# Products of zeros on TensorE between the first sixteen weight tiles, a later distance table and an earlier sum matrix

## The chip, the cores and the metric

The program runs on one core of one Trainium2 chip. The metric is the device time of one execution in microseconds. Before the change three timed runs took 1464.62, 1458.6 and 1463.09 us, so the median is 1463.09 us.

## What is computed

One inference step of a decoder of two layers, for a prompt of 256 tokens and 8 sample sequences of 8 tokens, with a model width of 1024. Everything is float32. What matters here is how a layer begins:

```python
def adaln(c, w, b):
    m = jax.nn.silu(c) @ w + b
    sh, sc, g = jnp.split(m, 3, axis=-1)
    return sh[:, None], sc[:, None], g[:, None]

def run_layer(x, c, mixer, w_ada_mix_l, b_ada_mix_l, w_in_l, ...):
    sh, sc, g = adaln(c, w_ada_mix_l, b_ada_mix_l)
    h = x * (1 + sc) + sh
    o, state = mixer(split_heads(h @ w_in_l))
...
```

No projection can start before the shift `sh` and the scale `sc` of the first layer are there. They are a product of the 9 conditioning vectors with 2048 of the 3072 columns of `w_ada_mix`, which is 8 MB of weights. A table of biases over distances (32 buckets times 16 heads) is also made once and is added to the logits of all attention maps later.

## The kernel before, in words

The five engines run programs of their own that meet at semaphores. Weights come as tiles of 512 KB. SP loads them in the order of the list `STREAM` into a ring of `RING = 4` slots; the load of tile n waits until tile n-4 has been used (`tile_used`).

**The front** is what stands ahead of the first projection. `FIRST` holds its 16 tiles. Tile n of it is counted from 0 here.

- POOL clears `cz`, then (L645 to L649) `epsc`, `qs`, `qi`, `wall`, `sel`, `selB`, `turnO`, `znew` and `sbias`, and signals `zeroed` once after `cz` and once at the end.
- ACT issues nine small loads (the list `first`, L713), the identity matrix first, then makes the exponential of the conditioning vectors. DVE makes silu of them into `cz` (L1407), padded with zeros to 32 columns.
- PE (`ada_tile`, L994) multiplies: for each tile two matmuls with 32 stationary columns of `cz` and 512 moving columns of the tile, each into a quarter of `bank[3]` by partitions. Two neighbouring tiles of a group of four use four different quarters.
- After each fourth tile ACT copies the bank to `adarow` (`ada_out`, L725), PE turns it in `ada_turn` (L1004: four products of a 128x128 piece of `adarow` with `sumG`, the 128x32 matrix that adds the quarters up), and DVE adds the bias into `adaT` (`ada_add`, L1447 and L1449).
- After tile 3 PE makes the distance table: three products of `relb` (34x16) with 1159 columns (L1025). It waits for all of `first`. DVE copies it out (L1419), and ACT writes it 16 times over to memory at the end of the front (`dist_sample`, L731), 1159 KB.
- `sumG` is made by DVE from the identity with three adds (L1409 to L1416), after a wait for all of `first`; the lambda terms (L1410, L1414) lie between these adds. ACT has the exponential of lambda (L717) ahead of its first `ada_out`.
- POOL and DVE make h of the first layer from `adaT` and x (L663, L666, L1526). PE then starts with the four tiles of `INDEX`: two together in `by_chunks` (L981, 16 matmuls), two in `chunk` (L972), then 16 matmuls with `wki` (L1044), and goes on with the list `PROJ`.

**SP around it** issues tiles 0 to 11, x, tiles 12 to 15, the four tiles of `INDEX` and `wki`. The load of the last `INDEX` tile waits for tile 15 of the front. Then, without any wait for PE, come the page numbers and the page loads of the indexer's keys (`load_ik(l, 0)`, L473), the nine constants (L535), `load_ik(l, 1)`, the loads of PROJ tiles 0 and 1, `load_ik(l, 2)`, and the loads of PROJ tiles 2 and 3. The load of PROJ tile 4 waits for PROJ tile 0 on PE. All of this is in program order, written out by hand.

Of the kernel before, what the change touches and what calls it, by code (L numbers as in the profile page):

```python
# [37 lines left out]
NCOND = 1 + NB  # L38
# [151 lines left out]
def repeat(ap, n):  # L190

    return bass.AP(ap.tensor, ap.offset, [*[list(x) for x in ap.ap], [0, n]])


def program(nc, a, out):
    ctx = ExitStack()
    with ctx:
# [3 lines left out]
        def sem(name):  # L201
            return ctx.enter_context(nc.semaphore(name))
# [38 lines left out]
              for x in (*(big[:, FF // P * T + PAST * s:FF // P * T + PAST * s + PAST] for s in range(6)),  # L241
# [52 lines left out]

        ld_cond = sem("ld_cond")
        ld_first = sem("ld_first")
        ld_x = sem("ld_x")
# [95 lines left out]

        first = [(ident[:], a["ident"]), (par_all[:, :, 0:P_NLAM], a["params"]),
                 (relb[0:32, :], a["rel_bias"]), (relb[32:34, :], a["relrows"]), (onehot, a["onehot"]),
# [50 lines left out]
        def _(sp):  # L446
# [74 lines left out]
            for l in range(DEPTH):  # L521
# [6 lines left out]
                if l == 0:  # L528

                    sp.wait_ge(ld_first, N_FIRST)  # L530
                    load_ik(l, 0)

                    sp.wait_ge(zeroed, 2)
# [107 lines left out]
        def _(pool):  # L641
# [3 lines left out]
            pool.memset(epsc[:], EPS)  # L645
            for t in (qs, qi, wall, sel, selB, turnO, znew, *sbias):
                pool.memset(t[:], 0.0)
# [61 lines left out]
        def _(act):  # L709
            for signal in (z_set, pd_relu, sd_relu, u_tset, up_relu, ln_x):  # L710
                act.sem_inc(signal.sem, signal.spare)
            for dst, src in first:
                act.dma_start(dst, src).then_inc(ld_first, 16)  # L713
            act.wait_ge(ld_cond, 16)
            act.activation(sgm[:], cT[:], ACT.Exp, scale=-1.0).then_inc(sig_exp, 1)
            act.wait_ge(lam_sum, 1)
            act.activation(ls[:], ls[:], ACT.Exp).then_inc(lam_exp, 1)  # L717

# [7 lines left out]

            ada_out(FIRST[3])
            for g in range(1, 4):
                ada_out(FIRST[4 * g + 3])
            act.wait_ge(dist_sb, 3)  # L730
            act.dma_start(dist_s, bass.AP(distb.tensor, distb.offset,  # L731
# [19 lines left out]
            load_ik(5)  # L751
            act.wait_ge(zeroed, 2)

# [196 lines left out]
        def _(pe):  # L950
# [57 lines left out]
            def sums(l, j):  # L1008
# [8 lines left out]
                          ).then_inc(ln_mm.sem, 1)  # L1017

            pe.wait_ge(silu_done, 1)
            for n, t in enumerate(FIRST):  # L1020
                ada_tile(t)
                if n == 3:
                    pe.wait_ge(ld_first, N_FIRST)
                    for c, (u0, u1) in enumerate(((0, 512), (512, 1024), (1024, NDIST))):
                        pe.matmul(bank[c][0:H, 0:u1 - u0], relb[:], big[0:34, u0:u1], start=True, stop=True  # L1025
                                  ).then_inc(dist_ps, 1)
                    pe.wait_ge(sum_set, 1)
                if n >= 4 and n % 4 == 0:
                    ada_turn(n // 4 - 1)
            ada_turn(3)  # L1030
            pe.wait_ge(zeroed, 2)

# [365 lines left out]
        def _(dve):  # L1398
# [7 lines left out]
            dve.wait_ge(zeroed, 1)  # L1406
            dve.tensor_tensor(cz[:, :, 0:NCOND], cT[:], sgm[:], ALU.mult).then_inc(silu_done, 1)  # L1407
            dve.wait_ge(ld_first, N_FIRST)
            dve.tensor_tensor(sumG[:], ident[:, 0:G], ident[:, G:2 * G], ALU.add)  # L1409
# [3 lines left out]
            dve.tensor_tensor(sumG[:], sumG[:], ident[:, 2 * G:3 * G], ALU.add)  # L1413
            dve.tensor_reduce(ls[:], lp, AX_X, ALU.add).then_inc(lam_sum, 1)  # L1414
            dve.drain()
            dve.tensor_tensor(sumG[:], sumG[:], ident[:, 3 * G:4 * G], ALU.add).then_inc(sum_set, 1)  # L1416
            for c, (u0, u1) in enumerate(((0, 512), (512, 1024), (1024, NDIST))):
# [3 lines left out]
            for l in range(DEPTH):  # L1421
# [10 lines left out]
                dve.memset(par_all[0:3 * G, l, P_COEF:P_COEF + 1], 1.0)  # L1432
            dve.wait_ge(zeroed, 2)
# [3 lines left out]
            def ada_add(t):  # L1437

                kind, l, i = t
                j, q = (1 if kind == "mlp" else 0), i // 4  # L1440
                dve.wait_ge(ada_tp, ada_group(t) + 1)
                to = adaT[:, 2 * l + j, 4 * q:4 * q + 4, :]
                ps = bank[4][:, 0:4 * G].rearrange("p (c n) -> p c n", n=G)[:, :, 0:NCOND]
                b0 = P_ADA + 24 * j + 4 * q
                bias = repeat(par_all[:, l, b0:b0 + 4], NCOND)
                if q < 2:
                    ins = dve.tensor_tensor(to, ps, bias, ALU.add)  # L1447
                else:
                    ins = dve.scalar_tensor_tensor(to, ps, 1.0, bias, ALU.add, ALU.add)  # L1449
                ins.then_inc(ada_set, 1)  # L1450

            for g in range(4):
                ada_add(FIRST[4 * g + 3])
# [431 lines left out]
```

## Time and profile before

| What | Value |
|---|---|
| Median of three runs | 1463.09 us (1458.6 to 1464.62) |
| The profiled execution: its time | 1461.34 us |
| Its span in the trace | 1459.3 us |
| Mean granted clock of TensorE | 0.967 |
| PE busy | 1345.6 us, 92% of the span |
| DVE, ACT, POOL busy | 505.3, 287.1 and 62.6 us |
| DMA, mean | 249 GB/s |

All durations below are of the one profiled execution. Its time is 2.0 us above its span, for what lies around the program, and 1.75 us below the median of the timed runs. The front is about 43 us of it. In the rows PE is a matmul, PEld a load of stationary weights, SPq and ACTq the issuing of DMAs on SP and ACT. A float32 matmul appears as two records, so "x16" is eight matmuls.

### The profile page before, as it was taken

How to read it: one execution, taken by the hardware profiler on the slowest of the kernel's cores; microseconds unless marked ns; L12 is line 12 of the kernel's file. 1: busy time of each engine (PE TensorE's matmuls, PEld its weight loads, DVE VectorE, ACT ScalarE, POOL GpSimd, SP SyncE). 2: the span in 40 equal slices, each digit the busy share in tenths (PEclk: the TensorE clock that was granted, in tenths of full speed). 3: DMA queues.
4: the chain of work that ended last, by engine and by line, in shares of the span. 5: the costliest groups of instructions: out<-in, count | busy, mean ns of one | idle time of the engine just before them, and what ended most of it. 6: DMA issues, size and time to landing. Idle time of an engine off the chain costs nothing.

```text
span 1459.3 us, 23536 instructions
## 1 busy us (share of the span) xinstructions
PE 1345.6 (92%) x8190; PEld 852.3 (58%) x8190; DVE 505.3 (35%) x1319; ACT 287.1 (20%) x712; POOL 62.6 (4%) x271
## 2 busy tenths in 40 slices
PE   6989899988899999999999999998879899999996
PEld 2544356655565666566665543665546567767774
DVE  1102777863354011011112077777534611100113
ACT  0011123343213111000003112433432311000001
POOL 1100000000001000000001000000000100000000
PEclk7899999999899999999999999999989999999998
DMA  7788979999943676987672677899994536675663
GB/s 278 208 279 269 306 233 359 357 298 308 293 145 108 238 263 234 320 290 262 264 259 95 209 263 239 303 366 294 298 332 160 195 135 248 214 280 203 237 203 129
DMA packets 189567, 363.82 MB, mean 249 GB/s; under 512 B 22912, under 2 KB 140360, under 8 KB 187786
## 3 DMA queue, kind: packets, MB, share of 16 engines
q1 hardware_dynamic: 165200, 350.19, 69.8%
q10 hardware_dynamic: 24250, 12.14, 3.2%
q8 instruction: 66, 1.08, 0.3%
q14 instruction: 51, 0.42, 0.1%
HBM read 354.17 MB, written 58.40 MB: 283 GB/s over the span
## 4 chain that ended last, share of the span: by engine, by line
PE 67%; SPq 10%; DVE 6%; DMA 6%; issue 5%; DVEq 3%; ACT 2%; ACTq 1%; POOLq 0%; POOL 0%
PE psf L972 21%; PE psf L1383 18%; SPq L473 9%; DMA ring<-in_tiles 4%; PE psf L1260 4%; PE psf L1298 4%; PE psf L1366 3%; PE psf L994 2%; PE psf L981 2%; PE psf L1153 2%; PE psf L1196 2%; DVE m L1515 2%; DVEq L1518 1%; PE psf L1044 1%; PE psf L1295 1%
## 5 line engine op out<-in xcount | busy, mean ns | idle before, releaser
L972 PE MATMUL psf<-hT,ring 128*128 128x320 f32 x1440 | 399.8, 435 | 10.0 <-DMA ring<-in_tiles 8.6
L972 PEld LDWEIGHTS psf<-hT,ring 128*128 128x128 f32 x1440 | 270.3, 190 | 139.4 <-issue 17.8
L1383 PE MATMUL psf<-big,ring 128*128 128x320 f32 x1024 | 279.3, 434 | 2.2 <-DVE big L1731 2.1
L1383 PEld LDWEIGHTS psf<-big,ring 128*128 128x128 f32 x1024 | 193.4, 190 | 88.5 <-issue 4.2
L1731 DVE TENSOR_TENSOR big<-sq 128x320 f32<-128x320 f32 x64 | 31.5, 492 | 261.5 <-ACT sq L941 261.2
L1459 DVE TENSOR_SCALAR rstd<-psf,adaT 128x256 f32<-128x256 f32 x32 | 15.4, 483 | 248.4 <-PE psf L1383 233.3
L1515 DVE MAX8 m<-workbuf 64x8 f32<-64x1032 f32 x64 | 78.5, 1226 | 3.0
L1153 PE MATMUL psf<-big,qs 128*32 128x512 f32 x512 | 69.5, 633 | 8.7 <-issue 5.6
L1517 DVE MATCH_REPLACE8 workbuf<-m,workbuf 64x1032 f32<-64x1032 f32 x64 | 77.4, 1209 | 0.0
L941 ACT ACTIVATE sq<-psf 128x320 f32<-128x320 f32 x64 | 28.0, 438 | 249.7 <-PE psf L972 233.1
L903 ACT ACTIVATE sq<-xT 128x320 f32<-128x320 f32 x32 | 15.1, 470 | 307.1 <-DVE xT L1463 307.1
L994 PE MATMUL psf<-ring,cz 128*32 128x512 f32 x384 | 63.2, 673 | 13.2 <-DVE cz L1407 8.4
L1196 PE MATMUL psf<-big,ptbuf 128*32 128x128 f32 x2048 | 65.4, 282 | 9.5 <-DMA big<-in_pool_cv 9.5
L1260 PE MATMUL psf<-oT,ring 128*128 128x320 f32 x256 | 71.4, 435 | 2.1 <-DVE oT L1622 1.0
L1196 PEld LDWEIGHTS psf<-big,ptbuf 128*32 128x32 f32 x2048 | 56.6, 113 | 16.1 <-issue 14.2
L1298 PE MATMUL psf<-ring,hT 128*128 128x512 f32 x128 | 65.2, 633 | 0.0
L1260 PEld LDWEIGHTS psf<-oT,ring 128*128 128x128 f32 x256 | 48.0, 190 | 23.2 <-DVE xT L1463 1.7
L1571 DVE CUSTOM_DVE_ANT_0 S<-psf,sbias 128x1032 f32<-128x1032 f32 x32 | 39.4, 1233 | 58.8 <-PE psf L1159 50.6
L763 ACT ACTIVATE zT<-psf,zscale 128x320 f32<-128x320 f32 x40 | 20.8, 527 | 167.6 <-PE psf L972 119.7
L1366 PE MATMUL psf<-hT,big 128*128 128x320 f32 x128 | 38.3, 464 | 4.8 <-ACT hT L916 4.8
L1242 PE MATMUL psf<-wki,S 128*128 128x128 f32 x240 | 37.6, 302 | 2.9 <-DVE oT L1662 2.9
L1181 PE MATMUL psf<-ident,S 128*128 128x128 f32 x128 | 21.1, 289 | 19.5 <-DVE oT L1622 19.1
(170 smaller groups left out, 1210.6 us busy)
## 6 DMA issues: line engine op xcount, KB each, us to landing
ring<-in_tiles SPq DMA_DIRECT2D x288, 512.0 KB, 4.4
big<-in_cache_a SPq DMA_DIRECT2D x64, 768.0 KB, 7.3
out_cache_a<-in_cache_a SPq DMA_DIRECT2D x64, 768.0 KB, 5.8
big<-in_pool_bk SPq DMA_DIRECT2D x128, 192.0 KB, 3.6
big<-in_pool_bv SPq DMA_DIRECT2D x128, 192.0 KB, 4.4
big<-in_pool_cv SPq DMA_DIRECT2D x256, 64.0 KB, 4.0
big<-in_pool_ck SPq DMA_DIRECT2D x128, 64.0 KB, 4.3
big<-in_pool_ck ACTq DMA_DIRECT2D x128, 64.0 KB, 4.4
```

The source lines that it names most:

```text
L473: sp.dma_start(dst[:, j, :], pool[ds(at[j] + l * N_PHYS, 1), :, w0:w0 + dst.shape[2]] .rearrange("o p w -> (o p) w")).then_inc(signal, 16)
L972: ins = pe.matmul(ps[:, 0:T], ring[:, s, k, :], rhs[:, k, :], start=k == 0, stop=k == KD - 1)
L994: ins = pe.matmul(bank[3][G * g:G * g + G, :], cz[:, c, :], wide(s, kk), start=c < 4, stop=c >= 4)
L1153: ins = pe.matmul(psf[G * c:G * c + G, 512 * q:512 * q + w], qs[:, u.s, G * c:G * c + G], rhs, start=True, stop=not masked)
L1196: ins = pe.matmul(bank[3][G * c:G * c + G, 0:P], lhs, rhs, start=j == 0, stop=j == NPG)
L1260: ins = pe.matmul(wo_bank(m)[:, 0:T], ring[:, s, k, :], oT[:, AT_O[k], :], start=k == 0, stop=k == KD - 1)
L1298: ins = pe.matmul(bank[v_bank(g, tt)], hT[:, 2 * s + kk, P * tt:P * tt + P], wide(slot, kk), start=first, stop=last)
L1366: ins = pe.matmul(up_bank(m)[:, 0:T], spare[m][:, k, :], hT[:, k, :], start=k == 0, stop=k == KD - 1)
L1383: ins = pe.matmul(bank[6 + m % 2][:, 0:T], ring[:, s, k, :], uT[:, KD * q + k, :], start=q + k == 0, stop=q == 3 and k == KD - 1)
L1515: dve.max(m8[0:TS, 0, :], work)
L1517: dve.match_replace(work, m8[0:TS, 0, :], work, TAKEN)
L1571: dve.tensor_tensor_reduce(out=S[:, 0, :], in0=psf[:, 0:L], in1=sbias[u.second][:], scale=1.0, scalar=-3e38, op0=ALU.add, op1=ALU.max, acc ...
```

## The change

It has three parts.

1. PE gets products of zeros. `still(w)` multiplies `qs[:, 0, :]` (128x128) with w columns of `qi`, both just cleared, into `bank[7]`. Four of 512 columns stand ahead of tile 0, one of 256 ahead of each of the tiles 1 to 15, and two of 512 behind the last turn. POOL's clearing is cut in two so that `qs` and `qi` are signalled first; who waited for the second signal now waits for the third.
2. The distance table moves from behind tile 3 to behind tile 9 on PE. On DVE its copies move behind the first two `ada_add`, and the lambda terms go with them.
3. The identity has a semaphore of its own (`ld_ident`), and `sumG` is made as soon as it has landed. ACT makes the exponential of lambda behind the first `ada_out`.

```diff
+            act.dma_start(ident[:], a["ident"]).then_inc(ld_ident, 16)
             for dst, src in first:
                 act.dma_start(dst, src).then_inc(ld_first, 16)
             act.wait_ge(ld_cond, 16)
             act.activation(sgm[:], cT[:], ACT.Exp, scale=-1.0).then_inc(sig_exp, 1)
-            act.wait_ge(lam_sum, 1)
-            act.activation(ls[:], ls[:], ACT.Exp).then_inc(lam_exp, 1)
...
-            ada_out(FIRST[3])
-            for g in range(1, 4):
+            for g in range(4):
                 ada_out(FIRST[4 * g + 3])
+                if g == 0:
+                    act.wait_ge(lam_sum, 1)
+                    act.activation(ls[:], ls[:], ACT.Exp).then_inc(lam_exp, 1)
...
+            def still(w):
+
+                pe.matmul(bank[7][:, 0:w], qs[:, 0, :], qi[:].rearrange("p i s w -> p (i s w)")[:, 0:w], start=True, stop=True)
+
+            pe.wait_ge(zeroed, 2)
+            for _ in range(4):
+                still(512)
             pe.wait_ge(silu_done, 1)
             for n, t in enumerate(FIRST):
+                if n:
+                    still(256)
                 ada_tile(t)
-                if n == 3:
+                if n == 9:
                     pe.wait_ge(ld_first, N_FIRST)
                     for c, (u0, u1) in enumerate(((0, 512), (512, 1024), (1024, NDIST))):
                         pe.matmul(bank[c][0:H, 0:u1 - u0], relb[:], big[0:34, u0:u1], start=True, stop=True
                                   ).then_inc(dist_ps, 1)
+                if n == 4:
                     pe.wait_ge(sum_set, 1)
                 if n >= 4 and n % 4 == 0:
                     ada_turn(n // 4 - 1)
             ada_turn(3)
-            pe.wait_ge(zeroed, 2)
+            pe.wait_ge(zeroed, 3)
+            for _ in range(2):
+                still(512)
...
             dve.tensor_tensor(cz[:, :, 0:NCOND], cT[:], sgm[:], ALU.mult).then_inc(silu_done, 1)
+            dve.wait_ge(ld_ident, 16)
+            dve.tensor_tensor(sumG[:], ident[:, 0:G], ident[:, G:2 * G], ALU.add)
+            for g in range(2, 4):
+                dve.drain()
+                ins = dve.tensor_tensor(sumG[:], sumG[:], ident[:, G * g:G * g + G], ALU.add)
+            ins.then_inc(sum_set, 1)
             dve.wait_ge(ld_first, N_FIRST)
...
+            ada_add(FIRST[3])
+            ada_add(FIRST[7])
             for c, (u0, u1) in enumerate(((0, 512), (512, 1024), (1024, NDIST))):
                 dve.wait_ge(dist_ps, c + 1)
```

PE in the front before, from tile 0 to the first matmuls with h (L994 tiles, L1025 the distance table, L1004 turns, L981 `by_chunks`):

```order
L994 MATMUL psf<-ring,cz 32x512 x8
L1025 MATMUL psf<-big,relb 16x512 x2
L1025 MATMUL psf<-big,relb 16x135
L994 MATMUL psf<-ring,cz 32x512 x2
L1004 MATMUL psf<-sumG,adarow 128x32 x4
L994 MATMUL psf<-ring,cz 32x512 x8
L1004 MATMUL psf<-sumG,adarow 128x32 x4
L994 MATMUL psf<-ring,cz 32x512 x8
L1004 MATMUL psf<-sumG,adarow 128x32 x4
L994 MATMUL psf<-ring,cz 32x512 x6
L1004 MATMUL psf<-sumG,adarow 128x32 x4
L981 MATMUL psf<-hT,ring 128x320 x16
```

Tiles stand next to each other in up to four, with the table behind tile 3. The same place now, first from the start to the first turn (L1027 is `still`, L1000 a tile, L1010 a turn):

```order
L1027 MATMUL psf<-qi,qs 128x512 x4
L1000 MATMUL psf<-ring,cz 32x512 x2
L1027 MATMUL psf<-qi,qs 128x256
L1000 MATMUL psf<-ring,cz 32x512 x2
L1027 MATMUL psf<-qi,qs 128x256
L1000 MATMUL psf<-ring,cz 32x512 x2
L1027 MATMUL psf<-qi,qs 128x256
L1000 MATMUL psf<-ring,cz 32x512 x2
L1027 MATMUL psf<-qi,qs 128x256
L1000 MATMUL psf<-ring,cz 32x512 x2
L1010 MATMUL psf<-sumG,adarow 128x32 x4
```

No two tiles are neighbours any more. Further on, from the turn after tile 8 to the turn after tile 12 (L1040 is the distance table):

```order
L1010 MATMUL psf<-sumG,adarow 128x32 x4
L1027 MATMUL psf<-qi,qs 128x256
L1000 MATMUL psf<-ring,cz 32x512 x2
L1040 MATMUL psf<-big,relb 16x512 x2
L1040 MATMUL psf<-big,relb 16x135
L1027 MATMUL psf<-qi,qs 128x256
L1000 MATMUL psf<-ring,cz 32x512 x2
L1027 MATMUL psf<-qi,qs 128x256
L1000 MATMUL psf<-ring,cz 32x512 x2
L1027 MATMUL psf<-qi,qs 128x256
L1000 MATMUL psf<-ring,cz 32x512 x2
L1010 MATMUL psf<-sumG,adarow 128x32 x4
```

The table now stands between tiles 9 and 10. The order of the DMAs on SP is the same as before, and on ACT too.

## Rows read from the trace of the kernel before

**Rows 1.** The page: the granted clock by 40 slices, and the loads of stationary weights

```profile
PEclk7899999999899999999999999999989999999998
...
L972 PEld LDWEIGHTS psf<-hT,ring 128*128 128x128 f32 x1440 | 270.3, 190 | 139.4 <-issue 17.8
```

**Rows 2.** Windows of 5 us: length, busy us by engine, then PEclk, DMA share, GB/s

```profile
20.00:25.00 5.00, 4.30 (x17) 1.09 (x18) 0.20 (x1) 0.60 (x1) 0.00 (x0) 0.50 0.55 175
...
30.00:35.00 5.00, 3.43 (x16) 0.75 (x10) 0.00 (x0) 0.60 (x1) 0.00 (x0) 0.78 1.00 414
35.00:40.00 5.00, 4.32 (x19) 1.14 (x18) 0.20 (x1) 0.60 (x1) 0.00 (x0) 0.66 0.86 283
...
45.00:50.00 5.00, 5.00 (x12) 3.25 (x11) 0.41 (x1) 0.00 (x0) 0.26 (x1) 0.58 1.04 201
```

**Rows 3.** Timeline of the front: start us, us, engine, line, op, [idle before <-releaser]

```profile
1.49 0.53 POOL L647 MEMSET qi<- 128x512 f32 x1
...
8.37 3.56 PE L994 MATMUL psf<-ring,cz 128*32 128x512 f32 x16 [8.37 <-DVE cz L1407]
9.23 0.18 PEld L994 LDWEIGHTS psf<-ring,cz 128*32 128x32 f32 x2 [0.66 <-issue]
10.08 0.24 PEld L994 LDWEIGHTS psf<-ring,cz 128*32 128x32 f32 x6 [0.67 <-issue]
...
13.89 2.88 PE L1025 MATMUL psf<-big,relb 34*16 34x512 f32 x6 [1.95 <-DMA zscale<-in_zscale]
...
16.70 1.92 PE L994 MATMUL psf<-ring,cz 128*32 128x512 f32 x4
...
20.40 3.63 PE L994 MATMUL psf<-ring,cz 128*32 128x512 f32 x12
...
21.25 0.18 PEld L994 LDWEIGHTS psf<-ring,cz 128*32 128x32 f32 x2 [0.66 <-issue]
22.11 0.18 PEld L994 LDWEIGHTS psf<-ring,cz 128*32 128x32 f32 x2 [0.67 <-issue]
...
33.63 1.05 PE L994 MATMUL psf<-ring,cz 128*32 128x512 f32 x4 [1.57 <-DMA ring<-in_tiles]
...
34.61 1.08 PE L1004 MATMUL psf<-sumG,adarow 128*128 128x32 f32 x8
...
35.62 3.70 PE L994 MATMUL psf<-ring,cz 128*32 128x512 f32 x12
...
39.37 0.60 ACT L725 ACTIVATE adarow<-psf 128x512 f32<-128x512 f32 x1 [6.67 <-PE psf L994]
...
43.34 11.77 PE L981 MATMUL psf<-hT,ring 128*128 128x320 f32 x32 [2.24 <-POOL hT L666]
```

**Rows 4.** What SP's queue waited for, 0 to 110 us: total us, times, longest

```profile
SPq L453 <- PE psf L994: 40.0, 14, 7.3
```

**Rows 5.** Timeline of SP's queue, 39.7 to 77 us

```profile
39.73 0.60 SPq L527 DMA_DIRECT2D wki<-in_wki  x1
45.17 10.13 SPq L473 DMA_DIRECT2D big<-in_pool_ik  x8
...
67.25 0.90 SPq L453 DMA_DIRECT2D ring<-in_tiles  x2
71.01 5.04 SPq L473 DMA_DIRECT2D big<-in_pool_ik  x8
76.09 0.91 SPq L453 DMA_DIRECT2D ring<-in_tiles  x2
```

**Rows 6.** DMA issues between 66 and 69 us: count, KB each, median us to landing

```profile
ring<-in_tiles SPq DMA_DIRECT2D x2, 512.0 KB, 4.2
```

**Rows 7.** Timeline of PE behind the front, at the full clock

```profile
72.36 4.57 PE L972 MATMUL psf<-hT,ring 128*128 128x320 f32 x16
...
106.13 1.07 PE L994 MATMUL psf<-ring,cz 128*32 128x512 f32 x8
...
140.70 1.98 PE L1298 MATMUL psf<-ring,hT 128*128 128x512 f32 x4
```

More of the change, by code:

```diff
@@ L295, in program @@
         ld_cond = sem("ld_cond")
+        ld_ident = sem("ld_ident")
         ld_first = sem("ld_first")
@@ L392, in program @@
         block = ctx.enter_context(nc.Block())
-        first = [(ident[:], a["ident"]), (par_all[:, :, 0:P_NLAM], a["params"]),
+        first = [(par_all[:, :, 0:P_NLAM], a["params"]),
                  (relb[0:32, :], a["rel_bias"]), (relb[32:34, :], a["relrows"]), (onehot, a["onehot"]),
@@ L531, in _ @@
                     load_ik(l, 0)
[L533 removed]
+                    sp.wait_ge(zeroed, 3)
                     for dst, src in consts:
@@ L645, in _ @@
             pool.memset(epsc[:], EPS)
-            for t in (qs, qi, wall, sel, selB, turnO, znew, *sbias):
+            for t in (qs, qi):
+                pool.memset(t[:], 0.0)
+            pool.drain()
+            pool.sem_inc(zeroed, 1)
+            for t in (wall, sel, selB, turnO, znew, *sbias):
                 pool.memset(t[:], 0.0)
@@ L751, in _ @@
             load_ik(5)
-            act.wait_ge(zeroed, 2)
+            act.wait_ge(zeroed, 3)
             for l in range(DEPTH):
@@ L1412, in _, with ada_add @@
             dve.drain()
-            dve.tensor_tensor(sumG[:], sumG[:], ident[:, 2 * G:3 * G], ALU.add)
             dve.tensor_reduce(ls[:], lp, AX_X, ALU.add).then_inc(lam_sum, 1)
-            dve.drain()
-            dve.tensor_tensor(sumG[:], sumG[:], ident[:, 3 * G:4 * G], ALU.add).then_inc(sum_set, 1)
+            def ada_add(t):
+                kind, l, i = t
+                j, q = (1 if kind == "mlp" else 0), i // 4
+                dve.wait_ge(ada_tp, ada_group(t) + 1)
+                to = adaT[:, 2 * l + j, 4 * q:4 * q + 4, :]
+                ps = bank[4][:, 0:4 * G].rearrange("p (c n) -> p c n", n=G)[:, :, 0:NCOND]
+                b0 = P_ADA + 24 * j + 4 * q
+                bias = repeat(par_all[:, l, b0:b0 + 4], NCOND)
+                if q < 2:
+                    ins = dve.tensor_tensor(to, ps, bias, ALU.add)
+                else:
+                    ins = dve.scalar_tensor_tensor(to, ps, 1.0, bias, ALU.add, ALU.add)
+                ins.then_inc(ada_set, 1)
+            ada_add(FIRST[3])
+            ada_add(FIRST[7])
             for c, (u0, u1) in enumerate(((0, 512), (512, 1024), (1024, NDIST))):
@@ L1432, in _ @@
                 dve.memset(par_all[0:3 * G, l, P_COEF:P_COEF + 1], 1.0)
-            dve.wait_ge(zeroed, 2)
+            dve.wait_ge(zeroed, 3)
             heads = ident[:, 0:3 * G].rearrange("p (c r) -> p c r", r=G)[:, :, 0:2 * NT]
             dve.tensor_copy(turnO[:, 0:6 * NT].rearrange("p (c r) -> p c r", r=2 * NT), heads)
[L1437 to L1452, printed above, removed]
+            for g in range(2, 4):
                 ada_add(FIRST[4 * g + 3])
```

1 line of the change is left out of this document (removed).

## The prediction

> **What bounds the kernel now.** I read the page first. TensorE has the full clock nearly everywhere, but the first digit of its clock line is a 7 [rows 1], so the front is one place where clock is missing. The windows show where: the granted clock, as a share of 2.4 GHz, is 0.50 at 20 to 25 us, 0.66 at 35 to 40 and 0.58 at 45 to 50 [rows 2]. A level of 0.50 is 1.2 GHz.
>
> The timeline of the front gives the price of each level. Three tiles took 3.63 us at 20.40, at half clock; the next start behind a single tile came 0.98 us later at the full clock (33.63 to 34.61) and 1.85 to 1.92 us later at half (16.70). A turn took 1.01 us at full (34.61 to 35.62) [rows 3]. The very first tiles ran at half clock too, although no level is on record there: their weight loads follow 0.85 us apart (9.23, 10.08), exactly as at 21.25 and 22.11 [rows 3]. So what the reader should see is a PE that is slow, not one that is short of work: SP's queue waited 40.0 us for the tiles of the front to be used [rows 4], and the DMA share was 0.55 at 20 to 25 us [rows 2]. Only tile 12 was waited for, 1.57 us at 33.63 [rows 3].
>
> Then I followed SP. Its load of the last INDEX tile waits for tile 15, which ends at 39.32 (35.62 + 3.70), and wki follows at 39.73 [rows 3, 5]. From there it reads page numbers and issues small loads without a pause that PE could shorten, until it issues PROJ tiles 0 and 1 at 67.25 and PROJ tiles 2 and 3 at 76.09 to 77.00 [rows 5]. PE ends PROJ tile 0 at 76.93 (72.36 + 4.57) [rows 7]. The two meet within 0.1 us. This is the fact on which my forecast rests: a chain of waits that is followed back from the end passes through PE here, but SP is as late by itself. What PE gains ahead of 76.9 counts only as far as SP gains it as well.
>
> **The change, part by part.**
>
> *The sum matrix and the table.* Before, PE stood still from about 11.9 to 13.89 us for the last small load [rows 3]. Both waits for it go from this place: the table moves behind tile 9, by when the load has long landed, and sumG needs the identity alone, which is issued first. Nothing new waits in its stead, since tiles 4 to 7 can be loaded while four spaced tiles run. The moved table costs PE the same columns. Its 2.88 us were partly at half clock [rows 3]; 1159 columns at the price of a 512-column matmul (1.98 for two, 0.99 each [rows 7]) are 2.2 us, so 2.2 to 2.9, and I take 2.2. DVE's copies and the lambda terms move into its idle time, and ACT's exponential lies behind a copy instead of ahead of it; the bound for these is nothing to 0.2 us each, and I take nothing, because PE is then 6 us of tiles away from needing either engine.
>
> *The start.* qs and qi are cleared by 2.02 us (1.49 + 0.53 [rows 3]), so the four products start at 2.1 us. At the full clock they take 4 x 0.99, ending at 6.1, under the 8.37 at which cz is ready. All four at half would take 4 x 1.85 (a single 512-column pair at half) and end at 9.5. I take 8.9, since before too the clock had risen during the tiles that started at 8.37: the table's first matmuls at 13.89 were already faster than its last.
>
> *The tiles.* With a still between them, two tiles can no longer share the array: two side by side take 1.0 us at the full clock (106.13, 1.07 with the pipeline's end [rows 7]), one alone takes 0.98 [rows 3]. A still of 256 columns is half of 0.99, 0.50. The sum at full clock, in us:
>
> - start 8.9
> - 16 tiles x 0.98 = 15.7
> - 15 stills x 0.50 = 7.5
> - 3 turns x 1.01 = 3.0
> - the table 2.2
> - 3 waits for ACT's copy: 0.60 and 0.1 for its signal, less the still beside it, 0.2 each = 0.6
> - end of tile 15: 37.9 us, against 39.32 now
>
> So the front's last tile comes 1.4 us earlier. The stills eat most of what the clock gives: bare tiles at the full clock would be 7.5 us earlier still. The bounds: at 0.86 for a tile and 0.43 for a still (pure streaming, if the 1.05 of a record holds 0.2 of pipeline) the end is 34.9, 4.4 us earlier than now; with 9.5 at the start, a wait of 1.57 at tile 12 as before and a table of 2.9, it is 40.8, 1.5 us later.
>
> A rule speaks against the stills. The rows show weight loads of 190 ns for 128 columns, two to a matmul [rows 1], and yet eight matmuls of 320 columns in 4.57 us [rows 7], with the loads hidden. The Trainium skill (TensorE: Matmul & The Clock Gate, Part 3, "The mechanism") says that weight loads overlap with matmuls in flight only when they go to other rows of the array. By that rule each still would show its two loads, 2 x 0.19 us, and the sum would be 15 x 0.38 = 5.7 us longer. The rows of the projections disagree with it for like shapes; no row shows a full-width matmul between two of 32 columns.
>
> *Behind the last tile.* ACT's copy, the turn, the bias and h take the same as now, 39.32 to 43.34, 4.0 us. The two stills fill 1.98 us of it at the full clock and end 0.2 us before h is there; at half they would end 1.7 us late. by_chunks took 11.77 us [rows 3], partly at half clock [rows 2]. At 0.57 for a matmul (4.57 for eight [rows 7]) it takes 9.1, so PE gains 2.7 more and reaches PROJ tile 0 at 72.36 - 1.4 - 2.7 = 68.3. But that tile is issued at 67.25 and lands 4.2 us later [rows 5, 6], 71.45, or 70.05 when SP is 1.4 us earlier. PE waits, ends the tile at 74.6, and SP comes to PROJ tiles 2 and 3 at 76.09 - 1.4 = 74.7 on its own. Everything behind follows SP. The 2.7 us of by_chunks are worth nothing; their cover is SP's chain of issues, and without it they count in full.
>
> The sum: 1461.34 - 1.4 = **1459.9 us** against the profiled execution, 3.2 below the median of the three runs (1463.09), of which the profiled execution itself lies 1.75 below. A measurement of this kernel can tell about 0.5%, 7.3 us, from no change.
>
> **The rivals.**
>
> *PE's lead counts.* If SP's issues between 45 and 67 us are slow only because of what else is in flight (eight page loads took 10.13 us at 45.17 but 5.04 at 71.01 [rows 5]) and go faster in the new phase, by_chunks counts: 1.4 + 2.7; with the streaming prices for tiles and stills 3.0 more. 1461.34 - 7.1 = 1454.2. Against it: the order and the number of these DMAs are unchanged.
>
> *The clock falls at tile 12.* Before, PE waited 1.57 us, did tile 12 and a turn at the full clock, and was back at half for the next three tiles, 3.70 us as against 3.63 [rows 3]. The change keeps this place: x is loaded ahead of tile 12, ACT's copy and a turn are next to it. Four tiles and three stills at half cost 4 x 0.87 + 3 x 0.50 = 5.0, the turn 0.9: 1459.9 + 5.9 = 1465.8.
>
> *Weight loads show* (the rule above): 1459.9 + 5.7 = 1465.6.
>
> *Zeros do not hold the clock* (the other side, and also the case that the change does not do what it says). If products of zeros leave TensorE at 1.2 GHz, every still is pure cost: 16 x 1.87 + 15 x 1.0 + 3 x 1.9 + 3.9 for the table + 9.5 at the start = 64 us for tile 15, 25 us later than now, and the time is 1486. It decides early: a tile and a still together cost 1.4 us more at half, so the gain is gone after one such pair, and the time is slower by more than 0.5% after eight of the sixteen. For it: the full clock came back before only at the end of runs of tiles with no turn in them. Against it: the full clock was held through tiles, turns and short waits around 106 us [rows 7], and stills use more of the array than tiles do.
>
> **How the numbers follow.** My forecast, with its bounds of -4.4 to +1.5, has 0.52; PE's lead counts 0.20; the clock falls at tile 12 0.13; weight loads show 0.07; zeros do not hold the clock 0.08. The forecast's own range is 1457 to 1463. The range for eight in ten takes in the first rival and both cases near 1466, and leaves out the last: 1453.5 to 1466.5. Against a median of 1463.1, faster by over 0.5% means under 1455.8: three quarters of the first rival and a little of the forecast, 0.17. Slower by over 0.5% means over 1470.4: the last rival and a little more, 0.09. The rest, 0.74, is within 0.5%.
>
> **What would show it.** In the new profile tile 15 should end at 35 to 39 us; stills should follow each other by 0.43 to 0.50 us beside their tile's 0.98; the granted clock should be 1.00 from 9 us to the end of by_chunks; by_chunks should take 9 us and PE should then stand still for about 2 us ahead of PROJ tile 0, waiting for the ring. SP's issue of PROJ tiles 2 and 3 should have moved by as much as tile 15. I am wrong if that wait is missing and the end moves by over 4 us, or if tiles follow at 1.9 us.

## The result, and the profile after

The change made the kernel a little slower. The median of 22 runs is 1464.92 us (1456.95 to 1470.23), that of the kernel before, run beside it 22 times, 1461.34 us (1454.17 to 1468.86). The ratio is 1.0023, with an interval of 1.0012 to 1.0034. The profiled execution took 1460.41 us, its span is 1458.2 us and its mean granted clock 0.973: by luck it is the third quickest of the 22, and 0.9 us quicker than the profiled execution before. So one pair of traces can't show this loss, and the count of runs matters more here than any single view.

The page after: the clock line, the queue that brings the engines' code, and the loads of stationary weights, which answer to [rows 1].

```profile
PEclk9999999999899999999999999999989999999998
...
q8 instruction: 66, 1.08, 0.3%
...
L978 PEld LDWEIGHTS psf<-hT,ring 128*128 128x128 f32 x1440 | 272.2, 191 | 140.2 <-issue 19.0
```

The windows of [rows 2] after, with one from behind the front (length, busy us of PE, PEld, DVE, ACT, POOL, then PEclk, DMA share, GB/s):

```profile
20.00:25.00 5.00, 4.93 (x26) 2.17 (x26) 0.20 (x1) 0.60 (x1) 0.00 (x0) 1.00 0.88 295
30.00:35.00 5.00, 4.83 (x25) 1.95 (x24) 0.55 (x4) 0.60 (x1) 0.00 (x0) 1.00 0.91 338
35.00:40.00 5.00, 4.30 (x21) 1.45 (x18) 0.00 (x0) 0.60 (x1) 0.00 (x0) 1.00 0.80 263
45.00:50.00 5.00, 5.00 (x21) 3.50 (x20) 0.00 (x0) 0.00 (x0) 0.00 (x0) 1.00 1.01 167
...
70.00:75.00 5.00, 3.98 (x9) 2.71 (x10) 0.00 (x0) 0.00 (x0) 0.00 (x0) 0.66 0.83 266
```

The zeros do hold the clock: it was 1.00 from 6 us, where the record of it begins, where the windows of [rows 2] had 0.50 to 0.78. The first window below 1.00 is the one at 70 us.

PE's timeline after, from the start to PROJ tile 0 (L1027 a product of zeros, L1000 a tile, L1040 the table, L1010 a turn, L987 `by_chunks`):

```profile
2.12 5.62 PE L1027 MATMUL psf<-qi,qs 128*128 128x512 f32 x8 [2.12 <-POOLq L649]
8.27 1.05 PE L1000 MATMUL psf<-ring,cz 128*32 128x512 f32 x4 [0.53 <-DVE cz L1425]
9.25 0.70 PE L1027 MATMUL psf<-qi,qs 128*128 128x256 f32 x2
9.88 1.05 PE L1000 MATMUL psf<-ring,cz 128*32 128x512 f32 x4
...
22.33 1.05 PE L1000 MATMUL psf<-ring,cz 128*32 128x512 f32 x4
...
25.82 2.12 PE L1040 MATMUL psf<-big,relb 34*16 34x512 f32 x6
...
31.96 1.05 PE L1000 MATMUL psf<-ring,cz 128*32 128x512 f32 x4 [0.17 <-DMA ring<-in_tiles]
...
37.69 1.05 PE L1000 MATMUL psf<-ring,cz 128*32 128x512 f32 x4
39.44 1.08 PE L1010 MATMUL psf<-sumG,adarow 128*128 128x32 f32 x8 [0.70 <-ACT adarow L729]
40.35 1.96 PE L1027 MATMUL psf<-qi,qs 128*128 128x512 f32 x4
42.15 8.78 PE L987 MATMUL psf<-hT,ring 128*128 128x320 f32 x32
...
71.02 6.16 PE L978 MATMUL psf<-hT,ring 128*128 128x320 f32 x16 [2.76 <-DMA ring<-in_tiles]
...
104.41 1.06 PE L1000 MATMUL psf<-ring,cz 128*32 128x512 f32 x8
```

Compared with [rows 3]: the last tile starts at 37.69 and ends one spacing of 0.98 later, at 38.67, 0.65 us earlier than before. `by_chunks` starts 1.19 us earlier and takes 8.78 us instead of 11.77. Then PE stands still for 2.76 us for PROJ tile 0, and does that tile in 6.16 us instead of 4.57 [rows 7], because the clock fell at the end of that wait (0.50 from 70.9 us for 3.4 us). It ends at 77.2, where it ended at 76.93 before. The last row answers to the one at 106.13 of [rows 7]: there the kernel is 1.72 us ahead.

SP's queue after, which answers to [rows 5]:

```profile
39.15 0.43 SPq L528 DMA_DIRECT2D wki<-in_wki  x1
43.43 11.05 SPq L474 DMA_DIRECT2D big<-in_pool_ik  x8
...
67.19 0.90 SPq L454 DMA_DIRECT2D ring<-in_tiles  x2
70.94 3.96 SPq L474 DMA_DIRECT2D big<-in_pool_ik  x8
74.94 0.91 SPq L454 DMA_DIRECT2D ring<-in_tiles  x2
```

SP issues PROJ tiles 0 and 1 only 0.06 us earlier, and tiles 2 and 3 1.15 us earlier. So the front did roughly what was foretold of it, up to 106 us. The medians differ by 3.6 us. These are lost behind it, where the program is the same.

### The profile page after: what moved, and what is told of

The parts are those of the page before. It is cut to its first block, busy times and chain, and to the rows that moved or that the text cites. A ratio compares the mean times of both kernels' runs of the same rounds, so it can differ in the third digit from the quotient of the medians.

```text
span 1458.2 us, 23623 instructions
## 1 busy us (share of the span) xinstructions
PE 1357.5 (93%) x8232; PEld 858.2 (59%) x8232; DVE 505.6 (35%) x1319; ACT 286.9 (20%) x712; POOL 62.8 (4%) x271
## 3 DMA queue, kind: packets, MB, share of 16 engines
q8 instruction: 66, 1.08, 0.3%
## 4 chain that ended last, share of the span: by engine, by line
PE 66%; SPq 12%; DVE 6%; DMA 5%; issue 5%; DVEq 3%; ACT 2%; ACTq 1%
PE psf L978 21%; PE psf L1401 18%; SPq L474 10%; DMA ring<-in_tiles 5%; PE psf L1278 4%; PE psf L1316 4%; PE psf L1000 3%; PE psf L1384 3%; PE psf L1171 2%; DVE m L1538 2%; PE psf L1214 2%; DVEq L1541 1%; PE psf L987 1%; SPq L466 1%; PE psf L1313 1%
## 5 line engine op out<-in xcount | busy, mean ns | idle before, releaser
L1000 PE MATMUL psf<-ring,cz 128*32 128x512 f32 x384 | 60.6, 604 | 2.9 <-DMA ring<-in_tiles 1.8
L769 ACT ACTIVATE zT<-psf,zscale 128x320 f32<-128x320 f32 x40 | 20.7, 527 | 169.6 <-PE psf L978 128.8
L1316 PEld LDWEIGHTS psf<-ring,hT 128*128 128x128 f32 x128 | 22.9, 199 | 29.9 <-issue 29.9
```

The source lines that it names most:

```text
L1000: ins = pe.matmul(bank[3][G * g:G * g + G, :], cz[:, c, :], wide(s, kk), start=c < 4, stop=c >= 4)
L1316: ins = pe.matmul(bank[v_bank(g, tt)], hT[:, 2 * s + kk, P * tt:P * tt + P], wide(slot, kk), start=first, stop=last)
```

## The experiments

Ratios are to the kernel before, run beside each on the same chip; its medians there were 1461.06, 1461.22, 1460.95 and 1461.96 us. All kernels compute the whole of the reference.

### One part at a time

`moves_only`: the change without any product of zeros.

```diff
-            pe.wait_ge(zeroed, 2)
-            for _ in range(4):
-                still(512)
...
-                if n:
-                    still(256)
...
-            for _ in range(2):
-                still(512)
```

> The change without any product of zeros: only the later table and the earlier sum matrix. If the stills are the loss (they keep the clock but cost 7.5 us of PE, and make PE run ahead of SP), this version is faster than the changed kernel by 3 us or more and at or below the kernel before, ratio 0.996 to 1.000. If the loss comes from the moved table or the lambda terms, it stays, ratio 1.001 to 1.004. Tile 15 should end earlier than 39.3 us by the 1.95 us that PE stood still for the last small load, if the clock stays as it was: about 37.4.

Measured: 1464.0 us, ratio 1.0001 (0.9979 to 1.0023). One run of 2717.6 us is left out of what is said below; without it the median is 1463.75. The tiles ran at half clock until 41 us, tile 15 ended at 41.8 and not at the expected 37.4, and `by_chunks` started at 45.03, 2.9 us later than after. The front without zeros is slower. The ratio is lower than that of the change, but its interval reaches into the other one, so this kernel alone doesn't part the two.

`stills_only`: the kernel before with all the products of zeros, without the two moves.

> The kernel before with all the products of zeros, the table and the sum matrix left where they were. If the stills carry the loss, the ratio is 1.001 to 1.004 as for the changed kernel. If only stills and moves together lose, it is 0.998 to 1.001. PE waits for the last small load behind tile 3 again, so tile 15 should end 1 us or less later than the 38.67 of the changed kernel (the stills before it end 5.5 us later than bare tiles would, and that covers the wait in part), and the clock should be full through the front unless that wait drops it.

Measured: 1470.2 us, ratio 1.0086 (1.0054 to 1.0118). The ratio is over the expected range. Two rows of its PE show where the front loses (L998 is a tile): tile 8, and tile 12 with its wait.

```profile
24.36 1.05 PE L998 MATMUL psf<-ring,cz 128*32 128x512 f32 x4
...
34.96 1.05 PE L998 MATMUL psf<-ring,cz 128*32 128x512 f32 x4 [3.19 <-DMA ring<-in_tiles]
```

The load of tile 12 waits for tile 8. With the table behind tile 3, tile 8 starts at 24.36; in the changed kernel, with the table behind tile 9, at 22.33, and tile 12 then waits 0.17 us instead of 3.19. After the wait of 3.19 us the clock was at half from 36 to 43 us. Tile 15 ended at 44.9 us, 6.2 later than after and not within the expected 1 us. So the moved table does a job of its own: it gives tile 8's slot back two microseconds sooner. The zeros need that move. (The table and the sum matrix went back together here; I tried neither alone. PE had no wait for the last small load.) `by_chunks` started at 48.36, 5.0 us later than in the kernel before, and the medians differ by 9.0: the front isn't the whole of this loss either.

`no_mid_stills`, `no_end_stills` and `end_stills_only`: the change without the 15 products between the tiles, without the last two, and with the last two alone.

> The changed kernel without the 15 products between the tiles; the four ahead and the two behind stay. If the clock holds without them, two tiles share the array again and tile 15 ends near 33 to 35 us, 4 us or more ahead of the changed kernel; by the theory that everything behind follows SP, which waits for tile 15, that gain is passed on in full, and the ratio is 0.996 to 0.999. If the clock falls without them, tile 15 ends at 37 to 42 us and the ratio is 1.000 to 1.003.

> The changed kernel without the two products behind the last turn. by_chunks falls back to half clock for some of its 16 matmuls and takes 10 to 11.8 us in place of 8.6. By the theory that PE's lead is swallowed by SP, PROJ tile 0 ends no later than the 77.1 us of the changed kernel, and the wait ahead of it is shorter, 0 to 1 us, so that the clock does not fall there: the ratio is equal to or lower than the changed kernel's, by 0 to 0.1%. If PE's lead counted, it would be higher by 0.15%.

> The moves with the two products behind the last turn alone. The front's tiles run mostly at half clock, tile 15 ends at 38 to 42 us as without any stills; by_chunks runs at the full clock if the stills do it alone, 8.6 us, else 10 to 11.8. If the loss belongs to PE running ahead of SP behind the front, it appears here too (ratio 1.002 or more); if it belongs to the stills between the tiles, the ratio is that of the moves alone, 1.000 to 1.001.

Measured: `no_mid_stills` 1461.73 us, ratio 0.9999 (0.9977 to 1.002); `no_end_stills` 1465.14, 1.002 (0.9992 to 1.0048); `end_stills_only` 1459.95, 0.9993 (0.9968 to 1.0018). PE in `no_mid_stills` behind the first four products of zeros:

```profile
8.36 1.91 PE L1000 MATMUL psf<-ring,cz 128*32 128x512 f32 x12
11.29 1.05 PE L1000 MATMUL psf<-ring,cz 128*32 128x512 f32 x4 [1.02 <-DMA ring<-in_tiles]
14.91 1.92 PE L1000 MATMUL psf<-ring,cz 128*32 128x512 f32 x4 [2.57 <-DMA ring<-in_tiles]
```

Three tiles side by side take 1.91 us at the full clock. PE then outruns the loads, waits 1.02 and 2.57 us, and is at half clock from 13.9 to 41.2 us; tile 15 ended at 41.9. The products between the tiles fill just that time. In `no_end_stills`, `by_chunks` took 10.54 us from 41.89, partly at half clock, where it takes 8.78 with them; but PE then waited 1.11 us for PROJ tile 0 instead of 2.76, the clock held, and the tile ended at 75.4 instead of 77.2. The two products at the end buy 1.5 us that are waited away, and in this trace the wait costs the clock.

`end_stills_only` shows what that is worth. It has the wait and the fall of the clock at the same place:

```profile
73.51 6.23 PE L978 MATMUL psf<-hT,ring 128*128 128x320 f32 x16 [2.74 <-DMA ring<-in_tiles]
```

Nearly the same row as after (6.16 us behind 2.76), and yet its ratio is 0.9993, where at least 1.002 was expected if PE's lead were the loss. So the loss goes with the products between the tiles, and not with the wait ahead of PROJ tile 0.

Taken together: with the moves in place, the kernels with the 15 products between tiles have the quicker front and the longer time. `stills_only`, which lacks the moves, has the slower front too.

### The wait at 71 us, and the changed kernel again

`tiles_early` issues the first two PROJ tiles ahead of layer 1's page loads, in the changed kernel; `before_tiles_early` does it in the kernel before; `again` is the changed kernel once more.

```diff
+                    for t in PROJ[l][:2]:
+                        load(t)
                     load_ik(l, 1)
...
                 for n, t in enumerate(PROJ[l]):
-                    load(t)
+                    if l or n > 1:
+                        load(t)
```

> The changed kernel with PROJ tiles 0 and 1 issued ahead of the page loads of the second sample sequence on SP, so 7 us earlier. By the theory that SP's chain of issues swallows what PE gains, the wait of 2.76 us ahead of PROJ tile 0 goes, with it the stretch at half clock from 71 to 75 us, and PROJ tile 0 ends at 72 to 73 us in place of 77.1. Behind it SP is still the bound until about 97 us, so the end moves by 0 to 2 us only; if the end moves by 4 us or more, the wait at PROJ tile 0 was the place where the gain of by_chunks went, and SP's later issues were not the bound.

> The kernel before with the same two loads issued earlier. There PE reached PROJ tile 0 without a wait, so PE gains nothing there: the same within 1 us at 77 us, ratio 0.998 to 1.002. If it is faster by 0.3% or more, the place of these loads matters by what it does to the queue and not by PE's wait.

> The changed kernel itself once more, for the size of the difference. Theory 1 (the loss is real, about 0.2%): the ratio to the kernel before is 1.001 to 1.004 again. Theory 2 (the 3.6 us between the medians are scatter): the interval holds 1.000. Both: tile 15 of the front ends at 38 to 39 us, and PE waits 2 to 3 us ahead of PROJ tile 0.

Measured: `tiles_early` 1462.6 us, ratio 1.0003 (0.9978 to 1.0028); `before_tiles_early` 1462.81, 1.0002 (0.9977 to 1.0027); `again` 1464.32, 1.0015 (0.9991 to 1.0038). The last interval holds 1.000, so `again` alone settles nothing. In `tiles_early` the wait was gone: PROJ tile 0 ran from 69.42 in 4.57 us. But PE then waited 2.16 us for a tile at 81.14, as SP now issues sixteen page loads in a row (65.91 to 76.68). Of 2.9 us gained at 77 us, 0.5 were left at 106. The wait was moved, not removed. The ratio of `tiles_early` can't tell whether the loss went with it: its interval holds both 1.000 and the 1.0023 of the change.

### Where TensorE's code is fetched

The traces gave another suspect. The queue q8 fetched code 66 times in both kernels, 1.08 MB, 16 KB each time; TensorE's program is 16860 instructions before and 16945 after, about 256 to a fetch. The fetches come at fixed places of the program. The 21 products of zeros (four instructions each) and one more wait add 85 instructions at the front, and so every later fetch falls on another piece of work. Of SP's DMA issues that took over 0.95 us, 29 of 36 before and 31 of 36 after have a fetch that began beside them or up to 1 us ahead; of the 1175 shorter ones only 43 and 45 have. A fetch was at 577.5 us after, and at 555.7 and 601.3 before. SP issues eight page loads there. After, SP's queue, then the issues of that tile between 573 and 586 us (duration ns min/median/max), and the queues between 577 and 579 us:

```profile
576.12 5.22 SPq L474 DMA_DIRECT2D big<-in_pool_ik  x8
```

```profile
L474 SPq DMA_DIRECT2D big<-in_pool_ik x8: 332/333/1537, 576.1 to 581.0; - x8
```

```profile
q8 instruction: 1, 0.02, 4.2%
```

One issue took 1537 ns where the others took 333. PE's wait for the next tile, after and then before:

```profile
585.22 10.01 PE L978 MATMUL psf<-hT,ring 128*128 128x320 f32 x30 [1.73 <-DMA ring<-in_tiles]
```

```profile
584.67 4.54 PE L972 MATMUL psf<-hT,ring 128*128 128x320 f32 x16 [0.49 <-DMA ring<-in_tiles]
```

Behind the wait of 1.73 us the granted clock was 0.66 from 585 to 590 us; before it was 1.00 there.

Four kernels shift the fetches with instructions that do nothing: 85 semaphore increments in the kernel before, ahead of its wait for silu; 171 (85 and 171 make 256) in the changed one, spread over the 16 matmuls of wki; the same with the tiles early; and 256 in the kernel before.

```diff
+            for _ in range(85):
+                pe.sem_inc(padded, 1)
             pe.wait_ge(silu_done, 1)
```

```diff
                     for k in range(KD):
+                        if l == 0:
+                            for _ in range(10 + (KD * (c - KI) + k < 11)):
+                                pe.sem_inc(padded, 1)
```

> The kernel before with 85 semaphore increments on TensorE where it waits for silu (it is idle there for over 7 us), so the front stays as it was. If the loss of the change comes from where TensorE's code is fetched (256 instructions to a fetch; the change adds 85 instructions), a fetch now lies near 577 us in SyncE's burst of page loads for the next layer's indexer, TensorE waits 1.4 to 2.0 us near 585 instead of 0.49 and its clock falls there for some 3 us, and the ratio to the kernel before is 1.001 to 1.004. If the loss comes from the products of zeros themselves, by the clock or the phase in which the layers meet it, the ratio is 0.999 to 1.001 and the wait near 585 stays 0.5 us.

> The changed kernel with 171 semaphore increments spread over the first layer's 16 matmuls of wki, so that the fetches behind about 70 us lie where they lay before (85 and 171 make 256). If the places of the fetches are the cause, the wait near 583 us goes from 1.73 us to about 0.5 without a fall of the clock, and the gain of the front shows: ratio 0.998 to 1.000. If not, the ratio stays at 1.0015 to 1.0025 as for the changed kernel, with the wait at 1.4 us or more.

> The same with the first two tiles of PROJ issued before layer 1's load of the indexer's keys, which took the wait of TensorE at 71 us away. By the places of the fetches: no wait over 1 us near 585 us, and a ratio of 0.997 to 1.000, at or a little under after_pad171. If the fetches are not the cause: 1.000 to 1.002, as tiles_early was.

> Control: the kernel before with 256 semaphore increments over the 16 matmuls of wki, one whole fetch more, so the later fetches lie where they lay. Expected by the places of the fetches: the wait near 585 us stays 0.5 us, ratio 0.999 to 1.001. If added instructions cost time by their number, wherever the fetches lie, it is over 1.001, and more than that of before_pad85.

Measured: `before_pad85` 1470.51 us, ratio 1.0082 (1.0053 to 1.0111); `after_pad171` 1470.93, 1.0071 (1.0043 to 1.0099); `tiles_early_pad171` 1474.62, 1.0093 (1.0062 to 1.0125); `before_pad256` 1487.9, 1.0199 (1.0167 to 1.0231). The ratio of all four was missed. The increments cost time themselves, which I had taken for nothing. In `before_pad85` the first tile started 6.5 us late, in `before_pad256` one matmul (two records) and its 16 increments took 2.44 us:

```profile
14.85 3.64 PE L995 MATMUL psf<-ring,cz 128*32 128x512 f32 x16 [14.85 <-issue]
```

```profile
61.50 0.78 PE L1048 MATMUL psf<-hT,wki 128*128 128x320 f32 x2 [1.22 <-issue]
63.94 1.04 PE L1048 MATMUL psf<-hT,wki 128*128 128x320 f32 x2 [1.67 <-issue]
```

That is 0.15 us for an increment (2.44 / 16). In `after_pad171` matmuls follow each other by 1.70 us with 11 increments between them and by 1.54 with 10, again 0.15 each. The semaphore's own records in the trace of `before_pad85` agree: the first increment is at 1.83 us, the last at 14.65, 0.151 apart. So 85 of them take 12.8 us. They began while PE stood idle, and the 6.5 us are what stuck out of the idle time. Three of these traces show PE at half clock as well, for 17.1 us from 67 us (`after_pad171`, `tiles_early_pad171`) and for 34.1 us from 64 us (`before_pad256`). The ratios say nothing on the fetches. The local half of the expectations held in all four: with the fetch in the burst PE waited 1.60 us, without it 0.65, 0.70 and 0.58.

### Fewer instructions for the same zeros

So the last four kernels shift the fetches by the zeros themselves. `bf16_pairs` has two products of bf16 zeros, 256 columns each, where one of float32 stood; it has as many instructions as the changed kernel. `bf16_stills` has one of 512 columns: 32 fewer (the expectations say 30). Both clear the tile `sel` early for it. `every_other` keeps the float32 products and has one of 512 columns ahead of every second tile: 28 fewer. `again2` is the changed kernel.

```diff
                 if n:
-                    still(256)
+                    for _ in range(2):
+                        pe.matmul(bank[7][:, 0:256], sel[:, 0:P], sel[:, 0:256], start=True, stop=True)
```

```diff
                 if n:
-                    still(256)
+                    pe.matmul(bank[7], sel[:, 0:P], sel[:, 0:512], start=True, stop=True)
```

```diff
-                if n:
-                    still(256)
+                if n % 2:
+                    still(512)
```

> Each product of zeros between tiles becomes two of bf16 zeros, 256 columns each: as many instructions as in the changed kernel (85 more than before). By the places of the fetches: the fetch stays near 577 us, TensorE waits 1.4 us or more near 583 us and its clock falls there; ratio 1.001 to 1.003. If the zeros' own time between tiles is the loss, it is shorter here (about 0.35 us a tile where it was 0.63): the front ends up to 4 us earlier, and the ratio is 0.998 to 1.000.

> The same with one bf16 product of 512 columns a gap: 30 instructions fewer (55 more than before), about the same work for TensorE. By the places of the fetches: the fetch near 577 us comes some 4.5 us later, behind SyncE's burst of page loads; the wait near 583 us falls to about 0.5 us without a fall of the clock, and the ratio is 0.002 lower than that of bf16_pairs (0.998 to 1.0005). If the fetches are not the cause: same as bf16_pairs within 0.0005, wait unchanged.

> The changed kernel with a product of 512 columns ahead of every second tile in place of one of 256 ahead of each: the same columns, 28 instructions fewer. By the places of the fetches: no wait over 1 us near 583 us and a ratio of 0.998 to 1.0005, provided the clock holds in the front. By the zeros' own time: 1.0015, as the changed kernel.

> The changed kernel itself, on the same chip as the three: ratio 1.001 to 1.003, the wait of 1.7 us near 583 us and the fall of the clock there.

| Kernel | Instructions added on TensorE | Median us | Ratio (interval) |
|---|---|---|---|
| `bf16_pairs` | 85 | 1466.45 | 1.004 (1.001 to 1.0069) |
| `again2` | 85 | 1466.35 | 1.0035 (1.001 to 1.006) |
| `bf16_stills` | 53 | 1462.99 | 1.0011 (0.9987 to 1.0035) |
| `every_other` | 57 | 1462.03 | 1.0004 (0.9978 to 1.003) |

The front does not order them. PE's rows in `bf16_pairs` (L1036 the zeros):

```profile
9.36 1.05 PE L1000 MATMUL psf<-ring,cz 128*32 128x512 f32 x4
10.35 0.39 PE L1036 MATMUL psf<-sel 128*128 128x256 bf16 x2
10.67 1.05 PE L1000 MATMUL psf<-ring,cz 128*32 128x512 f32 x4
```

Its tiles follow each other by 1.31 us, in the changed kernel by 1.61, and in `bf16_stills` by 1.31 too. Both bf16 kernels then waited for a tile at 32 us (2.43 and 1.77 us), dropped to half clock for 6.8 us, and started `by_chunks` at 44.72 and 44.32, two microseconds later than the changed kernel; `every_other` started it at 40.90. The first two differ by 3.5 us in the median with nearly the same front; the changed kernel (`again2`) and `every_other` by 4.3 us. Both pairs together differ by 4.9 us in the mean, with a standard error of 1.3. The traces of the first two part soon behind the front: at the matmul that stands at 106.13 us before, `bf16_stills` is at 104.83 and `bf16_pairs` at 110.94, behind a wait of 3.43 us for PROJ tile 0 and two stretches of 6.8 us at half clock. No run shows whether that place does so in other executions.

Over all batches, as means with their standard errors, in groups that I made after the runs: the kernel before 1461.4 +- 0.3 us (136 runs); with 1 to 25 instructions more (`moves_only`, `end_stills_only`, `no_mid_stills`) 1461.4 +- 0.7 (35 runs); with 53 and 57 more 1462.1 +- 0.8 (24 runs); with 85 more behind the moved table (`after`, `again`, `again2`, `bf16_pairs`, `tiles_early`) 1465.2 +- 0.5 (70 runs). The step of 3.1 us between the last two is three times its standard error of 1.0. (`no_end_stills`, 77 more, lies between: 1464.3 +- 1.4. `tiles_early` alone, 1463.2 +- 1.2, fits both.) Part of the scatter within a kernel is the clock: over the 46 runs of the changed kernel the quickest quarter has a mean granted clock of 0.975, the slowest 0.971.

The burst of eight page loads near 577 us and PE's wait behind it, in all eighteen traces:

| Kernels | Longest issue, ns | Burst, us | PE's wait, us |
|---|---|---|---|
| no fetch in it: before, `before_tiles_early`, `moves_only`, `end_stills_only`, `no_mid_stills`, `bf16_stills`, `after_pad171`, `tiles_early_pad171`, `before_pad256` | 342 to 345 | 4.02 to 4.03 | 0.42 to 0.73 |
| a fetch in it: after, `again`, `again2`, `tiles_early`, `no_end_stills`, `stills_only`, `bf16_pairs`, `every_other`, `before_pad85` | 984 to 1782 | 4.68 to 5.47 | 1.20 to 2.03 |

The groups don't touch. Here is the burst in `bf16_stills`, which answers to the rows of after above:

```profile
579.63 4.03 SPq L474 DMA_DIRECT2D big<-in_pool_ik  x8
```

```profile
587.70 4.54 PE L978 MATMUL psf<-hT,ring 128*128 128x320 f32 x16 [0.69 <-DMA ring<-in_tiles]
```

In seven of the nine kernels with the fetch the clock also fell to half for 3.4 us behind the wait, in none of the other nine. What the place costs in these traces can be read off, since the same PE work frames it in all of them: from the pair of tiles beside the burst to the next pair. Before, then after:

```profile
577.79 1.06 PE L994 MATMUL psf<-ring,cz 128*32 128x512 f32 x8
...
598.17 1.06 PE L994 MATMUL psf<-ring,cz 128*32 128x512 f32 x8
```

```profile
577.12 1.06 PE L1000 MATMUL psf<-ring,cz 128*32 128x512 f32 x8
...
600.00 1.07 PE L1000 MATMUL psf<-ring,cz 128*32 128x512 f32 x8
```

That is 20.4 us before and 22.9 after. It is 19.9 to 20.4 us in all nine kernels without the fetch, 22.5 to 23.2 in the seven with the fetch and the fall of the clock, and 20.7 in the two with the fetch alone. So the fetch by itself costs 0.3 to 0.8 us here, and 2.1 to 3.3 where the clock falls too. `bf16_stills` came out as foretold: no fetch in the burst, a short wait, a ratio 0.003 under that of `bf16_pairs`. `bf16_pairs` itself missed the other half of what was expected of it: PE waited 1.20 us there and not 1.4 or more, and the clock held. `every_other` hit its ratio and missed its mechanism: the fetch still fell into the burst and PE waited 1.23 us. It has no fall of the clock there; neither has `bf16_pairs`, which is slow all the same. So the place near 577 us does not sort the times by itself.

## Why the prediction was right and wrong

The forecast was 1459.9 us, a gain of 1.4 us on the profiled execution. Measured was a loss of 0.23%, inside the eight-in-ten range (1453.5 to 1466.5) and within the 0.5% that had most of the chance, but outside the forecast's own range of 1457 to 1463 and on the other side of zero.

- **The zeros hold the clock: right.** It was 1.00 from about 6 us to 70.9. `no_mid_stills` is the counter-test: half from 14 to 41 us.
- **The start: 0.6 us too late.** The four products ended at 7.74, and tile 0 started at 8.27 where I took 8.9.
- **The price of a product between tiles: wrong by a quarter.** Forecast 0.50 us, measured 0.63 (1.61 less 0.98), 15 x 0.13 = 2.0 us. A product of 512 columns among its like takes 0.86 us (its two loads start 0.43 us apart, at 6.29 and 6.72 in the trace after), one of 256 half of that, so each insertion costs 0.20 us beyond its columns. One product of 512 columns in `every_other` costs 1.06 us (8.72, 9.70, 10.76), again 0.20 more than its 0.86. That is about the length of one load of 191 ns that is not hidden; that it is the load isn't shown. The rule of the Trainium skill (TensorE: Matmul & The Clock Gate, Part 3, "The mechanism"), to which I gave 0.07, foretells a load of full height that shows between tiles; the trace agrees in kind. By two loads it would be 0.38 us, the trace shows half of it, and among products of one shape it shows the loads hidden, where the rule would let them show.
- **The table, the turns, the copies: right to 0.6 us together** (the table 2.05 us, where 2.2 was taken). The last tile ended at 38.67 instead of 37.9: 37.9 - 0.6 + 2.0 - 0.6 for the rest.
- **Behind the last tile: right.** `by_chunks` started 3.5 us behind it (forecast 4.0) and took 8.78 us (9.1).
- **"The 2.7 us of by_chunks are worth nothing": right in the trace**, and for the reason given. PE waited 2.76 us at PROJ tile 0, where about 2 were forecast. What I had not seen is that the wait would cost the clock: the tile took 6.16 us instead of 4.57, and PE, not SP, was last at 77 us (77.2 against 74.94). `no_end_stills` had 1.11 us of waiting, no fall and an end at 75.4. Even so the kernel was 1.72 us ahead at 106 us; up to there the forecast holds.
- **"Everything behind follows SP": the step that failed.** I took the 1380 us behind the front as a block that is shifted. It is not one: the same instructions met other waits and other fetches. In the trace after, one stretch of 20.4 us near 577 us took 22.9: the lead, 1.72 us at 106 us and 0.67 at the start of that stretch, was a lag of 1.83 at its end. (This one trace made it good later and ended 1.1 us ahead; the median run did not.) `end_stills_only` and `no_mid_stills` have a front 2.5 to 3.2 us later than the changed kernel's and a median 3 to 5 us shorter; `moves_only` has a front 2.9 us later and a median 0.9 us shorter, 0.3 us under that of `again` beside it.
- **What the loss is made of** is settled in part. Shown: it goes with the products of zeros between the tiles, and not with a later front or with the wait at 71 us (`end_stills_only`, `no_mid_stills`). Shown to nearly four standard errors: with fewer instructions for them it is smaller (`bf16_pairs` against `bf16_stills`, the changed kernel against `every_other`). Whether the number of instructions does it, or the places of the fetches that go with it, these kernels don't part. Shown: the added instructions shift TensorE's code fetches, and a fetch in SP's burst lengthens the burst by 0.7 to 1.4 us and PE's wait by some 0.5 to 1.5 us, 2.1 to 3.3 us of PE's time in all where the clock falls. Open: how much of the 3 us this one fetch makes. It can make nearly all of it where the clock falls too, but whether it falls there in most executions no run shows. `every_other` had the fetch without the fall and no loss that can be measured, within an interval of 0.25% either way; `bf16_pairs` had the same and is slow all the same. The rest may be other fetches among the 65 behind the front. The sum of PE's waits behind 90 us is 77 to 82 us in all unpadded traces, in no order that follows the medians; single traces scatter by as much as is sought. I tried no kernel with as many instructions, at no cost, and the fetches elsewhere.

None of the rivals was it. The first counted PE's lead, and PE's lead was waited away; the clock did not fall at tile 12 (0.17 us of wait); a cost of about half the loads did show, 3.0 us of front. That rival's time, 1465.6, lies within 0.7 us of the measured median by luck: the cost is already in the tile that ended at 38.67, and the loss came behind it.

## What to carry to other kernels

Filling an engine's waits with empty work bought the clock and 1.2 us of front here, but the front was not the bound at its end, and the kernels with the most instructions added lost about 3 us behind it, more than they gained: before adding any, ask what the next wait is worth and whether the same filling can be had with fewer instructions (half as many products, twice as wide, lost nothing that could be measured). A block of unchanged code is not a constant: for effects of 0.2% its time must be measured over dozens of runs, since here two single traces pointed the other way. When padding is used as a probe, measure the padding alone first.

## What was not expected of the hardware

- A semaphore increment on TensorE took 0.151 us. 85 of them, begun at 1.83 us in an idle time that ended at 8.37, lasted until 14.65, and the first tile came 6.5 us late.
- A fetch of TensorE's code (16 KB) that began up to 0.3 us ahead of one of SP's DMA issues came with an issue 984 to 1782 ns long near 577 us, against 333.
- A product with 128 stationary columns between two with 32 costs 0.20 us above its columns at the full clock; in bf16 a product of 512 columns there took 0.33 us in all (1.31 less 0.98), against 1.06 in float32.
- The clock fell to half behind waits of 2.76 us (after) and 2.11 us (`again`) and did not behind one of 3.55 us at the same place of the same kernel (`again2`), and it fell behind a wait of 1.73 us at 583 us. The length of a wait alone did not tell.
